# Attention stage: value rounding in two halves, and VectorE's remainders moved to ScalarE's step

## The reference

```python
kv = rmsnorm(h, kv_norm) @ w_kv                       # keys and values, 16 heads of 64
q = (rmsnorm(h, b_norm) @ w_q)                        # queries
for each chunk n of 64 positions:
    s = einsum("bqhd,bkhd->bhqk", q_n, k_band) * 64 ** -0.5 + bias
    s = where(valid, s, -1e30)
    p = softmax(s, axis=-1)
    o_n = einsum("bhqk,bkhd->bqhd", p, v_band)
h = h + o @ w_out
```

## Time and profile before

| | before |
|---|---|
| median of 3 runs | 1885.48 us |
| profiled execution, its own time | 1883.86 us |
| its span, first to last instruction | 1882.2 us |
| TensorE matmul busy | 1809.3 us, 96% |
| TensorE weight load busy | 1435.8 us, 76% |
| VectorE busy | 1197.2 us, 64% |
| ScalarE busy | 841.5 us, 45% |
| granted TensorE clock, mean | 0.990 |

### The profile page before, as it was taken

How to read it: one execution, slowest core, us unless ns; L and a number is a source line. 1 busy time by engine, 2 the same in 40 slices (tenths; PEclk the granted TensorE clock), 3 DMA queues, 4 the chain that set the end, 5 groups by cost and what they waited for, 6 DMA issues and landing times.

```text
span 1882.2 us, 24272 instructions
## 1 busy us (share of the span) xinstructions
PE 1809.3 (96%) x8358; PEld 1435.8 (76%) x8358; DVE 1197.2 (64%) x1908; ACT 841.5 (45%) x1352; POOL 34.4 (2%) x65
## 2 busy tenths in 40 slices
PE   9999999879999999999998999999999999899997
PEld 6777777657888888888886788888887776677875
DVE  7777777746777763357776576777433688655434
ACT  6444444434444442257777444444323365543222
POOL 1000000000000000000000000000001000000000
PEclk9999999999999999999999999999999999999999
DMA  5411211102222232133322322222321301212221
GB/s 202 146 56 58 60 61 34 67 23 101 94 95 89 98 108 96 56 126 110 110 76 62 123 93 96 89 98 74 126 92 49 106 30 67 95 67 99 90 89 57
DMA packets 44824, 163.26 MB, mean 87 GB/s; under 512 B 5873, under 2 KB 6148, under 8 KB 44768
## 3 DMA queue, kind: packets, MB, share of 16 engines
q1 hardware_dynamic: 39872, 148.00, 23.1%
q0 software_dynamic: 4464, 14.47, 2.7%
q10 hardware_dynamic: 432, 0.07, 0.0%
HBM read 155.89 MB, written 6.63 MB: 86 GB/s over the span
## 4 chain that ended last, share of the span: by engine, by line
PE 88%; DVE 5%; issue 3%; ACT 3%; DMA 0%; DVEq 0%; SPq 0%; ACTq 0%
PE acc L550 23%; PE acc L551 22%; PE acc L552 22%; PE acc L574 7%; PE pc L698 2%; PE pb L681 2%; DVE wsplit L1580 1%; ACT wsplit L1084 1%; PE pa L952 1%; PE pd L964 1%; PE pd L903 1%; PE pd L902 1%; PE pa L551 0%; PE pa L550 0%; PE pa L552 0%
## 5 line engine op out<-in xcount | busy, mean ns | idle before, releaser
L550 PE MATMUL acc<-xhi,wsplit 128*128 128x512 f32 x1200 | 497.9, 415 | 9.5 <-DVE wsplit L1580 7.4
L1084 ACT ACTIVATE wsplit<-wraw 128x1024 fp32r<-128x1024 f32 (+1 forms) x252 | 275.4, 1097 | 454.5 <-PE acc L552 418.6
L551 PE MATMUL acc<-xlo,wsplit 128*128 128x512 f32 x1200 | 476.2, 397 | 0.0
L552 PE MATMUL acc<-xhi,wsplit 128*128 128x512 f32 x1200 | 475.9, 397 | 0.0
L1580 DVE TENSOR_TENSOR wsplit<-wraw,wsplit 128x1024 fp32r<-128x1024 f32 (+1 forms) x252 | 319.9, 1273 | 140.4 <-ACT wsplit L1084 139.2
L550 PEld LDWEIGHTS acc<-xhi,wsplit 128*128 128x128 f32 x1200 | 226.6, 189 | 70.5 <-issue 11.8
L551 PEld LDWEIGHTS acc<-xlo,wsplit 128*128 128x128 f32 x1200 | 226.9, 189 | 55.4 <-issue 4.3
L552 PEld LDWEIGHTS acc<-xhi,wsplit 128*128 128x128 f32 x1200 | 226.3, 189 | 54.9
L574 PE MATMUL acc<-xhi,wsplit 128*128 128x512 f32 x464 | 154.7, 408 | 0.0
L552 PE MATMUL acc<-hid_hi,wsplit 128*128 128x512 f32 x352 | 139.5, 396 | 0.0
L550 PE MATMUL acc<-hid_hi,wsplit 128*128 128x512 f32 x352 | 139.5, 396 | 0.0
(11 more groups left out here) (351 smaller groups left out, 2685.0 us busy)
## 6 DMA issues: line engine op xcount, KB each, us to landing
wraw<-w SPq DMA_DIRECT2D x220, 512.0 KB, 3.3
wraw<-w SPq DMA_DIRECT2D x32, 704.0 KB, 4.2
bias_dram<-ext_dram POOLq DMA_DIRECT2D x1, 4096.0 KB, 20.9
bias<-bias_dram POOLq DMA_DIRECT2D x16, 256.0 KB, 3.2
at_ks<-at_ks SPq DMA_DIRECT2D x16, 256.0 KB, 2.9
crow<-row_dram POOLq DMA_DIRECT2D x8, 256.0 KB, 3.7
brow<-row_dram POOLq DMA_DIRECT2D x8, 256.0 KB, 4.5
outT<-h SPq DMA_DIRECT2D x8, 256.0 KB, 2.2
```

What stands on the lines that cost most here:

```text
L550: mm(out, whi[:, k, :], a[:, x_at + k, :], start=(k == first), stop=False)
L551: mm(out, whi[:, k, :], b[:, x_at + k, :], start=False, stop=False)
L552: m = mm(out, wlo[:, k, :], a[:, x_at + k, :], start=False, stop=(k == last))
L1084: A(split(s, j, 0), raw(s, j), ACT.Copy).then_inc(w_hi_ready, 1)
```

## The change

Three things change in the attention, and nothing elsewhere.

1. ScalarE's and VectorE's `turned_v`, one operation for both heads of a pair, becomes two, one for each head: 4x64 columns in each of 128 partitions in place of 8x64. The first stands at step 1 on both engines, the second at step 3. The second waits on ScalarE for the first one's remainder as well. Before, ScalarE's stood at step 2 and VectorE's at step 3.
2. On VectorE `head_lo` moves from steps 1, 2 and 5, 6 to steps 0, 1 and 4, 5, which are the steps in which ScalarE's `head_hi` stands. Its block is now ahead of the one with `take` and `low_ahead`, `take` loses its wait on `kq_lo_ready`, and the addition to `at_o` moves from steps 0 and 4 of the following group to steps 7 and 3, ahead of both.
3. On ScalarE the copy out of `pd` goes from behind `pt_hi` to the head of its step; `ob_hi` moves from step 4 to 3, `ob_lo` on VectorE from 5 to 4.

```diff
@@ TensorE, dense
-                            pe.wait_ge(ev("vt_lo_ready"), i)
+                            pe.wait_ge(ev("vt_lo_ready"), 2 * i)
@@ TensorE, ahead of the product with the values
-                        pe.wait_ge(ev("vt_lo_ready"), n // 2 + 1)
+                        pe.wait_ge(ev("vt_lo_ready"), n + 1)
@@ ScalarE
-                def turned_v(i):
+                def turned_v(i, e):
 
                     act.wait_ge(ev("at_v_turned"), i + 1)
+                    if e > 0:
+                        act.wait_ge(ev("vt_lo_ready"), 2 * i + 1)
                     if i > 0:
-                        act.wait_ge(ev("pv_done"), 2 * i)
-                    A(at_vs[:, :, :, 0, :], chunks(acc[:, 2, :]).rearrange("p t (e d) -> p t e d", e=2), ACT.Copy).then_inc(ev("vt_hi_ready"), 1)
+                        act.wait_ge(ev("pv_done"), 2 * i + e - 1)
+                    A(at_vs[:, :, e, 0, :], chunks(acc[:, 2, :])[:, :, 64 * e:64 * e + 64], ACT.Copy).then_inc(ev("vt_hi_ready"), 1)
...
-                for step in range(units + 6):
+                for step in range(units + 5):
                     i, r = step // 8, step % 8
+                    if 7 <= step < units + 4 and step % 4 == 3:
+                        n = (step - 7) // 4
...
+                        A(at_o[own, :], pd[64:P, :], ACT.Copy).then_inc(ev("at_o_steps"), 1)
                     if step < units:
...
-                    if 7 <= step < units + 4 and step % 4 == 3:
-                        n = (step - 7) // 4
...
-                        A(at_o[own, :], pd[64:P, :], ACT.Copy).then_inc(ev("at_o_steps"), 1)
                     if 0 < i < PAIRS:
                         if r in (0, 1):
                             head_hi(i, 1, r)
-                        if r == 2:
-                            turned_v(i)
+                        if r == 1:
+                            turned_v(i, 0)
+                        if r == 3:
+                            turned_v(i, 1)
...
-                    if step >= 12 and r == 4:
+                    if step >= 11 and r == 3:
@@ VectorE
-                    if i < PAIRS - 1:
-                        if r in (2, 5, 7):
-                            j = (2, 5, 7).index(r)
-                            dve.wait_ge(ev("kq_lo_ready"), 4 * i + 3 + min(j, 1))
-                            take(i + 1, j)
-                        if r in (5, 6):
-                            head_lo(i + 1, 0, r - 5)
-                        if r in (3, 6) and i < PAIRS - 2:
-                            low_ahead(s, i + 1, r // 3 - 1, False)
-                    if 0 < i < PAIRS:
-                        if r in (1, 2):
-                            head_lo(i, 1, r - 1)
-                        if r == 3:
-                            turned_v(i)
-                        if r == 0 and i < PAIRS - 1:
-                            low_ahead(s, i, 2, False)
-                    if 8 <= step < units + 5 and step % 4 == 0:
-                        n = (step - 8) // 4
+                    if 7 <= step < units + 4 and step % 4 == 3:
+                        n = (step - 7) // 4
                         own = slice(64 * (n % 2), 64 * (n % 2) + 64)
                         dve.wait_ge(ev("at_o_steps"), 2 * n + 1)
                         tt_(at_o[own, :], pd[0:64, :], at_o[own, :], ALU.add).then_inc(ev("at_o_steps"), 1)
+                    if 0 < i < PAIRS:
+                        if r in (0, 1):
+                            head_lo(i, 1, r)
+                        if r == 1:
+                            turned_v(i, 0)
+                        if r == 3:
+                            turned_v(i, 1)
+                        if r == 0 and i < PAIRS - 1:
+                            low_ahead(s, i, 2, False)
+                    if i < PAIRS - 1:
+                        if r in (2, 5, 7):
+                            take(i + 1, (2, 5, 7).index(r))
+                        if r in (4, 5):
+                            head_lo(i + 1, 0, r - 4)
+                        if r in (3, 6) and i < PAIRS - 2:
+                            low_ahead(s, i + 1, r // 3 - 1, False)
...
-                    if step >= 13 and r == 5:
+                    if step >= 12 and r == 4:
```

More of the change, by code:

```diff
@@ L1383, in attention @@
                 cast_ahead(s, 0, 2, False)
-                turned_v(0)
-                for step in range(units + 6):
+                turned_v(0, 0)
+                turned_v(0, 1)
+                for step in range(units + 5):
                     i, r = step // 8, step % 8
+                    if 7 <= step < units + 4 and step % 4 == 3:
+                        n = (step - 7) // 4
+                        own = slice(64 * (n % 2), 64 * (n % 2) + 64)
+                        act.wait_ge(ev("pv_done"), n + 1)
+                        if n >= 2:
+                            act.wait_ge(ev("ob_lo_ready"), n // 2 + 1)
+                        A(at_o[own, :], pd[64:P, :], ACT.Copy).then_inc(ev("at_o_steps"), 1)
                     if step < units:
@@ L1932, in head_lo, with turned_v @@
                     tt_(lo, [at_k, at_q][j][own, :], hi.bitcast(F32), ALU.subtract).then_inc(ev("kq_lo_ready"), 1)
[L1934 to L1938, removed]
+                def turned_v(i, e):
+                    dve.wait_ge(ev("vt_hi_ready"), 2 * i + e + 1)
+                    tt_(at_vs[:, :, e, 1, :], chunks(acc[:, 2, :])[:, :, 64 * e:64 * e + 64], at_vs[:, :, e, 0, :].bitcast(F32),
+                        ALU.subtract).then_inc(ev("vt_lo_ready"), 1)
                 dve.wait_ge(ev("rstd_ready"), n)
```

## The result

The changed kernel takes 1916.51 us (median of 4 runs, 1914.99 to 1919.4) against 1885.0 for the one before, run beside it: a ratio of 1.0169 (95% interval 1.0151 to 1.0185), slower by 31.5 us. Direction and mechanism were forecast; the size was put at 22.1, and the range ended at 1915, so the measured time lies above it. The profiled execution took 1914.14 us, its span is 1912.5.

The account below looks back on a forecast made before the run. TensorE set the pace before; afterwards ScalarE and VectorE taking turns would. Twelve four-step stretches added 18.2 us and the next 4.0, summed as +22.1 on 1885.48: 1907.6 us, range 1901 to 1914, or 1896 to 1915 with half of one rival.

Parts of the forecast that it names:

- the ring: Second layer's attention: ScalarE and VectorE alternate instead of overlapping, as head_lo precedes the next bias; 75 in 100, 1901 to 1914.
- the value wait: TensorE's wait for VectorE's at_vs: five times, growing to about 0.9 us each.
- Twelve legs: Four-step stretches between probabilities-times-values matmuls (L902), twelve from the first: 167.7 us against 149.53, +18.2.
- leg B: From the L902 matmul of step 6 to the next pair's at step 2: 13.42 us against 12.46.
- leg A: From the L902 matmul of step 2 to that of step 6 in a pair: 14.69 us against 12.46.
- The leg after PV 12: Four steps after the twelve summed stretches, with the output's second split: 13.2 to 13.4 us against 9.16, +4.0.
- The last two legs and the end: Last attention stretches, no head_lo left, then the same chain to the next stage's matmul: booked 0, bounds -1.4 and +2.
- a single fall: Granted clock falling once around 1030 us, after two closely following waits of about 2 us: worth 2.5 us at most.
- Faster (1): Rival: early halves pay, the 2.35 us and 1.4 us waits both go: 1881.7 us; 5 in 100.
- Leg A only (2): Rival: only the stretch from step 2 to step 6 lengthens: 1898.6 us, or 1896.6 without the end; 11 in 100.
- The clock once a pair (3): Rival: granted clock falls once per pair, 7 times 2.5 us: +17.5, 1925 us; 6 in 100.
- Names only (4): Rival: VectorE reaches the bias in time because ScalarE runs earlier as well; within 0.3%; 3 in 100.

Follow-up runs that it names:

- the first experiment: Changed kernel with VectorE's head_lo put back one step, behind the next bias; value halves, at_o and ob_hi stay as changed: 1893.46 us, ratio 1.0048.
- the second experiment: Kernel before the change with head_lo alone moved into ScalarE's step, ahead of the next bias: 1916.04 us, ratio 1.0167.
- the splits first: Changed kernel with VectorE's weight splits of steps 0 and 3 moved ahead of the operations that wait there: 1905.69 us, ratio 1.0114.

## Why the prediction was right in kind and too small

- *What bounds.* Right: TensorE before, the ring after. Putting head_lo back, moving it alone and shortening what stands behind it each changed the time as a ring does.
- *The ring.* Right in place and order; every wait that I named is there: pt_lo 13 times, exponents for the bias, at_ks and at_qs for ScalarE, the value wait grown from 1.0 to 4.8 idle. With head_lo alone moved the loss is whole, with head_lo put back 23 of 31.5 us go.
- *Its size: the step that failed.* The terms of the ring were too short, those in which one operation follows another. I had written that a ready operation starts 0.10 (ScalarE) or 0.08 (VectorE) before the end of the last and that a hand-over takes 0.03, and applied it to every term. Twelve legs came to 174.25 us (855.07 to 1029.32) instead of 167.7: +24.7, not +18.2. In leg B, from pt_hi at 948.71 to PV: pt_hi to at_ks 0.51 for 0.39, at_ks to split 0.71 for 0.60, pt_hi to at_qs 0.60 for 0.50, at_qs to value half 0.71 for 0.60, and both hand-overs of head_lo 0.10 for 0.03. That is 0.12 + 0.11 + 0.10 + 0.11 + 0.14 = 0.58 of the 0.7 by which the leg exceeds 13.42. In leg A at_o, the exponent and pt_hi behind it, and the bias behind at_qs are late by 0.50 together and the hand-overs by 0.13; two places that I had taken 0.12 too long offset 0.24 of it, which leaves the 0.4 measured. The late starts all touch the upper 64 partitions or come behind one that does; for ScalarE's pt_hi the exchange of pd's halves shows that this is the cause, for the others the rows agree with it. Why the hand-over to head_lo takes 0.10 stays open.
- *It could have been read before.* In the earlier trace rows at_o of 0.59 is followed after 0.62, and I put in 0.50; exponent and copy (1.13) hold 0.12 of the same kind, and I put them in as a block, though in the changed kernel's leg A, without at_o ahead of them, they take 1.01 (964.04 to 965.05). On an engine with slack this costs nothing; on the ring it is added once per place.
- *The leg after PV 12.* +4.0 by my sum, 13.95 - 9.16 = +4.8 measured. It is a leg B, which elsewhere was 0.7 longer than summed.
- *The last two legs and the end.* From PV 13 to the first matmul after the stage has 20.16, here 21.41: +1.25 where I booked 0 (bounds -1.4 and +2). The granted clock is 0.84 over 1038 to 1042 and 0.50 in 1042 to 1046, so it fell at about 1040.7, behind the wait of 2.07 and when the one of 2.48 had just begun. Without head_lo in the ring (the first experiment), with one wait of 2.10 in the leg before, the clock stays at 1.00 and the same leg is 8.8 us:

```profile
1023.32 0.51 PE L902 MATMUL pd<-pt_hi,at_vs 128*128 128x512 f32 x1 [2.10 <-DVE pt_lo L1976]
...
1032.16 0.40 PE L902 MATMUL pd<-pt_hi,at_vs 128*128 128x512 f32 x1
```

Against 1053.21 - 1043.27 = 9.94 here, the fall costs about 1.1. In the three other runs with head_lo in VectorE's early place (the second experiment, the splits first, pd's halves exchanged) the clock falls near the stage's end too, and this leg is 9.8 to 9.95. I had named a single fall there and left it inside the range, but booked nothing for it.
- *Rivals.* Faster (1): no; splitting the values helped nothing, alone it costs 9 us. Leg A only (2): no, leg B is 14.1 for 12.46. The clock once a pair (3): no, 1.00 in all steady stretches at 87% busy; once at the end: yes. Names only (4): no.
- *Halves.* 0.38 and 0.42 us measured for the half-size value operations, 0.38 and 0.41 taken.

- *Slips in the sums, too small to matter.* 18.2 and 4.0 are 22.2, not 22.1. Rival 2 counts five legs A and leaves out the sixth (13.7 - 12.46 = 1.3). The ring's own range, by its terms, is 1902.2 to 1914.6, not 1901 to 1914; of these terms +3 stood for hand-overs, and the legs were 7.3 longer than summed.

Together 24.7 + 4.8 + 1.25 is 30.8 where I had 22.1; the first PV came 0.4 earlier, which leaves 30.4.

## What to carry to other kernels

Where two engines pass work back and forth in lists of fixed order, look at what stands between an operation that waits for the partner's newest result and the operation for which the partner waits next: one step of distance lets both overlap, none puts their times in series, even when each engine is only 75% busy before. Moving a remainder "as early as it can be ready" is the wrong aim when it stands ahead of the partner's input. When a ring is summed from a trace, take starts to starts of the same two operations on the same partitions: four such places, 0.1 us each, were 0.44 of the 0.7 us by which leg B was longer than summed, and a slip of that size comes back in every leg.

## What the runs showed of the hardware

- A start held back by the partitions. ScalarE and VectorE start an operation 0.07 to 0.12 us before the printed end of the last, or 0.02 to 0.04 behind it when it reads from, or writes to, another start partition (0 or 64) than the last read or write of the same memory, SBUF or PSUM. The Trainium skill (VectorE: DVE Perf Modes, Two Vector instructions with no wait between them) models this for VectorE: an instruction is held until all earlier ones are done when an input or its output starts in another quadrant (a group of 32 partitions) than the last read or write of that memory. The traces agree, at_ks of the lower against the upper head above, and the exchange of pd's halves shows the same on ScalarE.
- The granted clock fell from 1.00 to 0.50 at about 1040.7 us of the changed kernel, after waits of 1.69, 0.85, 0.30 and 2.07 us ahead of the matmuls at 1029.32, 1033.06, 1035.41 and 1038.83. It stayed at 1.00 in the steady stretches, with one wait of 1.4 us in each leg B and waits of 0.95, 0.23 and 1.03 in each leg A, and in the first experiment, where the longest wait in 1010 to 1030 was 2.10.
- A hand-over to head_lo took 0.10 us in all its 28 waits, to at_o or ob_lo 0.03. In the code head_lo has two waits in front and the others one; whether that is why was not tried.
